# Gate stage of a hybrid decoder block: y transposed by DMA in 16-bit planes instead of by TensorE

## What is computed

```python
proj = hn @ w_in
q, k, v, z, xbc, dt_raw, gate_logits = jnp.split(proj, split_points, axis=-1)
...
y = ssd_chunked(...) + xs * d_skip
y = y * silu(z)                                  # (256 tokens, 4096)
yg = y.reshape(bsz, seq, 8, 512)                 # 8 groups
yg = yg * lax.rsqrt(jnp.mean(jnp.square(yg), axis=-1, keepdims=True) + EPS)
y = yg.reshape(...) * norm_w
y_ssm = y @ w_ssm_out                            # needs y transposed
gates = jax.nn.sigmoid(gate_logits)
h = h + (g_attn * y_attn + g_ssm * y_ssm) @ w_out
h = h + jnp.square(relu(rms_norm(h) @ w_up)) @ w_down
```

## Time and profile before

| what | us |
|---|---|
| median of 3 runs | 2055.06 (2054.35 to 2055.19) |
| profiled execution, its own time | 2054.75 |
| its span, first to last instruction | 2052.7 |
| TensorE busy | 2041.6 (99%) |
| VectorE, ScalarE, GpSimd busy | 1216.3, 1037.7, 189.4 |
| raw loads of w_in | 319 of 512 KB |

### The profile page before, as it was taken

How to read it: one execution, slowest core, us unless ns; L and a number is a source line. 1 busy time by engine, 2 the same in 40 slices (tenths; PEclk the granted TensorE clock), 3 DMA queues, 4 the chain that set the end, 5 groups by cost and what they waited for, 6 DMA issues and landing times.

```text
span 2052.7 us, 27154 instructions
## 1 busy us (share of the span) xinstructions
PE 2041.6 (99%) x9374; PEld 1694.7 (83%) x9374; DVE 1216.3 (59%) x1346; ACT 1037.7 (51%) x1238; POOL 189.4 (9%) x210
## 2 busy tenths in 40 slices
PE   9999999999999999999999999999999999999999
PEld 8888888888888888888888888888888888888887
DVE  5665566666666666666655555555545555554654
ACT  6454555555565454545554444455435534534542
POOL 2110010000012111111210000000000000000000
PEclk9999999999999999999999999999999999999999
DMA  7656555656665655666555556567667666666765
GB/s 241 186 164 183 166 167 171 178 176 179 178 201 177 194 194 184 196 198 190 174 183 185 193 187 225 194 185 223 203 193 211 213 193 202 204 210 194 201 218 163
DMA packets 231213, 394.08 MB, mean 192 GB/s; under 512 B 45776, under 2 KB 46736, under 8 KB 230880
## 3 DMA queue, kind: packets, MB, share of 16 engines
q1 hardware_dynamic: 229712, 389.54, 62.0%
q10 hardware_dynamic: 960, 2.75, 0.4%
q0 software_dynamic: 464, 0.77, 0.2%
HBM read 382.46 MB, written 2.16 MB: 187 GB/s over the span
## 4 chain that ended last, share of the span: by engine, by line
PE 97%; DVE 1%; ACT 1%; issue 0%; DMA 0%; DVEq 0%; ACTq 0%
PE ps L485 31%; PE ps L487 31%; PE ps L486 30%; PE ps L454 2%; PE ps L710 1%; ACT whi L849 0%; PE ps L562 0%; PE ps L539 0%; PE ps L699 0%; DVE f_st L1682 0%; DVE fT_lo L1690 0%; PE ps L720 0%; DVE cacc L1462 0%; ACT fT_hi L1236 0%; DVE wlo L1268 0%
## 5 line engine op out<-in xcount | busy, mean ns | idle before, releaser
L1268 DVE TENSOR_TENSOR wlo<-raw,whi 128x1024 fp32r<-128x1024 f32 x703 | 892.2, 1277 | 669.1 <-ACT whi L849 667.4
L849 ACT ACTIVATE whi<-raw 128x1024 fp32r<-128x1024 f32 x703 | 736.5, 1058 | 645.5 <-PE ps L487 628.6
L485 PE MATMUL ps<-whi,xT_hi 128*128 128x512 f32 x1276 | 509.5, 399 | 0.0
L487 PE MATMUL ps<-whi,xT_lo 128*128 128x512 f32 x1276 | 498.1, 390 | 0.0
L486 PE MATMUL ps<-wlo,xT_hi 128*128 128x512 f32 x1276 | 496.9, 389 | 0.0
L487 PEld LDWEIGHTS ps<-whi,xT_lo 128*128 128x128 f32 x1276 | 239.5, 188 | 51.3
L486 PEld LDWEIGHTS ps<-wlo,xT_hi 128*128 128x128 f32 x1276 | 240.0, 188 | 47.8 <-issue 1.0
L485 PEld LDWEIGHTS ps<-whi,xT_hi 128*128 128x128 f32 x1276 | 239.8, 188 | 47.8 <-issue 1.3
L485 PE MATMUL ps<-whi,fT_hi 128*128 128x512 f32 x512 | 199.6, 390 | 3.3 <-DVE fT_lo L1690 3.3
L485 PE MATMUL ps<-whi,hT_hi 128*128 128x512 f32 x512 | 199.3, 389 | 0.0
L487 PE MATMUL ps<-whi,fT_lo 128*128 128x512 f32 x512 | 199.2, 389 | 0.0
(11 more groups left out here) (254 smaller groups left out, 1856.7 us busy)
## 6 DMA issues: line engine op xcount, KB each, us to landing
raw<-in_w_in SPq DMA_DIRECT2D x319, 512.0 KB, 3.8
raw<-in_w_up SPq DMA_DIRECT2D x128, 512.0 KB, 4.1
raw<-in_w_down SPq DMA_DIRECT2D x128, 512.0 KB, 4.3
raw<-in_w_ssm_out SPq DMA_DIRECT2D x64, 512.0 KB, 4.2
raw<-in_w_attn_out SPq DMA_DIRECT2D x32, 512.0 KB, 4.3
raw<-in_w_out SPq DMA_DIRECT2D x32, 512.0 KB, 4.4
arow<-arows SPq DMA_DIRECT2D x16, 512.0 KB, 4.9
h<-in_x ACTq DMA_DIRECT2D x1, 2048.0 KB, 12.0
```

Source lines behind the costliest of these rows:

```text
L485: mm(dst, xh, whi[sl][:, kk, :], start=(s == 0 and kk == 0), stop=False)
L487: last = mm(dst, xl, whi[sl][:, kk, :], start=False, stop=(s == US - 1 and kk == UK - 1))
L849: A(whi[s % SLOTS][:, :, :], raw[s % SLOTS][:, :, :], ACT.Copy).then_inc(hi_ready, 1)
L1268: V.tensor_tensor(wlo[s % SLOTS][:, :, :], raw[s % SLOTS][:, :, :], fp(whi[s % SLOTS][:, :, :]), ALU.subtract).then_inc(lo_ready, 1)
```

## The change

The eight groups of y go the MLP's way. `y_halve(G)` on ScalarE copies the two 16-bit planes of xs[G] into `y_half`; `y_turn(G, a)` on SyncE transposes plane a into `y_tiles`; `y_join(G)` on VectorE puts the planes together into `yT`, from which `s_hi` and `s_lo` read, with the norm weights from `par`. There is one buffer of each, so `y_halve(G)` waits for both turns of group G - 1, a turn of G for the join of G - 1, and `y_join(G)` for the lo parts of G - 1.

Where they stand, with jb the gate block: ScalarE does s_hi(2jb - 1) and y_halve(2jb) in step 0, y_halve(2jb + 1) and s_hi(2jb) in step 4; VectorE s_lo(2jb - 1) in step 0, y_join(2jb) in step 3, s_lo(2jb) in step 5, y_join(2jb + 1) in step 7. SyncE issues the first turn of group 2jb behind the load of unit 7 of block jb, its second behind unit 0 of the next block, and both turns of group 2jb + 1 behind units 4 and 5 of that. TensorE's transposes and GpSimd's `y_copy` are gone. The gate blocks are written out instead of looped on ScalarE, VectorE and SyncE, and so is SyncE's first pair of SSM blocks.

```diff
@@ -142,3 +142,5 @@
         la = sb("la", "W", 1 * KB, [P, NTOK, SNH])
-        y_st = [sb(f"y_st{i}", "W", 4 * KB * i, [P, NTOK, GW]) for i in range(2)]
+        y_half = sb("y_half", "W", 0, [P, 2, NTOK, GW], u16)
+        y_tiles = sb("y_tiles", "W", 4 * KB, [P, 2, NTOK * 4, P], u16)
+        yT = sb("yT", "W", 8 * KB, [P, 4, T])
         blank = sb("blank", "W", 4 * KB, [P, P])
...
@@ -365,3 +367,21 @@
 
-            def load_block(b, w, row0, col0, turn=None):
+            def y_turn(G, a):
+                sp.wait_ge(y_halved, G + 1)
+                if G:
+                    sp.wait_ge(y_joined, G)
+                else:
+                    sp.wait_ge(ysq_done, 16)
+                sp.dma_start_transpose(y_tiles[:, a, :, :], y_half[:, a, :, :].rearrange("p t n -> p (t n)")) \
+                    .then_inc(y_turned, 16)
+
+            def gate_turns(jb, s):
+
+                if jb and s == 0:
+                    y_turn(2 * jb - 2, 1)
+                if jb and s in (4, 5):
+                    y_turn(2 * jb - 1, s - 4)
+                if jb < 4 and s == 7:
+                    y_turn(2 * jb, 0)
+
+            def load_block(b, w, row0, col0, gate=None, turn=None):
 
@@ -374,2 +394,4 @@
                         r_turn(turn, s - US + 2)
+                    if gate is not None:
+                        gate_turns(gate, s)
 
@@ -424,5 +446,7 @@
                 ssd_loads(j1)
-            with sp.Fori(0, 4) as j:
-                load_block(B_GATE + j, w_in, 0, GATE0 + D + j * COLS)
-            with sp.Fori(0, 4) as j:
+            for j in range(4):
+                load_block(B_GATE + j, w_in, 0, GATE0 + D + j * COLS, gate=j)
+            load_block(B_SSM, w_ssm_out, 0, 0, gate=4)
+            load_block(B_SSM + 1, w_ssm_out, D, 0)
+            with sp.Fori(1, 4) as j:
                 load_block(B_SSM + 2 * j, w_ssm_out, 0, j * COLS)
@@ -743,18 +767,5 @@
 
-            def y_transposes(G, i):
-                def f():
-                    pe.wait_ge(y_copied, G + 1)
-                    for c in range(4):
-                        for t in range(NTOK):
-                            o = (c % 2) * T + t * P
-                            last = transpose(ps[4 + 2 * i + c // 2][:, o:o + P], y_st[i][:, t, c * P:(c + 1) * P])
-                    last.then_inc(y_T, 1)
-                return f
-
             with pe.Fori(0, 2) as i:
                 for k in range(2):
-                    jb = 2 * i + k
-                    G = 2 * jb
-                    stream(B_GATE + jb, k, 18 + i, xT_hi, xT_lo,
-                           after={2: [y_transposes(G, 0)], 6: [y_transposes(G + 1, 1)]})
+                    stream(B_GATE + 2 * i + k, k, 18 + i, xT_hi, xT_lo)
 
@@ -1142,16 +1153,26 @@
 
-            def s_hi(G, i):
+            def y_halve(G):
+                def f():
+                    act.wait_ge(yfin, 2 * G + 2)
+                    if G:
+                        act.wait_ge(y_turned, 32 * G)
+                    else:
+                        act.wait_ge(y_mm, 16)
+                    A(y_half[:, :, :, :].rearrange("p a t n -> p a (t n)"),
+                      halves(xs[:, G, :, :].rearrange("p t n -> p (t n)")), ACT.Copy).then_inc(y_halved, 1)
+                return f
+
+            def s_hi(G):
                 def f():
-                    act.wait_ge(y_T, G + 1)
+                    act.wait_ge(y_joined, G + 1)
                     for c in range(4):
-                        A(sT_hi[:, bass.ds(4 * G + c, 1), :].rearrange("p a t -> p (a t)"),
-                          ps[4 + 2 * i + c // 2][:, (c % 2) * T:(c % 2 + 1) * T], ACT.Copy,
-                          scale=sw[i][:, c:c + 1]).then_inc(sT_hi_done, 1)
+                        kt = 4 * G + c
+                        A(sT_hi[:, kt, :], yT[:, c, :], ACT.Copy,
+                          scale=par[:, SSM_C + kt:SSM_C + kt + 1]).then_inc(sT_hi_done, 1)
                 return f
 
-            with act.Fori(0, 2) as i:
-                for k in range(2):
-                    jb = 2 * i + k
-                    steps(B_GATE + jb, {2: [s_hi(2 * jb, 0)], 6: [s_hi(2 * jb + 1, 1)],
-                                        7: [sgate_evac(B_GATE + jb, k, jb)]})
+            for jb in range(4):
+                steps(B_GATE + jb, {0: ([s_hi(2 * jb - 1)] if jb else []) + [y_halve(2 * jb)],
+                                    4: [y_halve(2 * jb + 1), s_hi(2 * jb)],
+                                    7: [sgate_evac(B_GATE + jb, jb % 2, jb)]})
 
@@ -1163,2 +1184,4 @@
                         act.wait_ge(m_step, 3 * j)
+                    else:
+                        act.wait_ge(y_turned, 32 * 8)
                     for t in range(NTOK):
@@ -1176,3 +1199,3 @@
 
-            steps(B_SSM, {7: [half_evac(0)]})
+            steps(B_SSM, {0: [s_hi(7)], 7: [half_evac(0)]})
             steps(B_SSM + 1)
@@ -1594,17 +1617,25 @@
 
-            def s_lo(G, i):
+            def y_join(G):
                 def f():
-                    for half in range(2):
-                        dve.wait_ge(sT_hi_done, 4 * G + 2 * half + 2)
-                        for cc in range(2):
-                            c = 2 * half + cc
-                            V.scalar_tensor_tensor(
-                                sT_lo[:, bass.ds(4 * G + c, 1), :].rearrange("p a t -> p (a t)"),
-                                ps[4 + 2 * i + half][:, cc * T:(cc + 1) * T], sw[i][:, c:c + 1],
-                                fp(sT_hi[:, bass.ds(4 * G + c, 1), :].rearrange("p a t -> p (a t)")),
-                                ALU.mult, ALU.subtract).then_inc(sT_lo_done, 1)
+                    dve.wait_ge(y_turned, 32 * G + 32)
+                    if G:
+                        dve.wait_ge(sT_lo_done, 4 * G)
+                    for a in range(2):
+                        i = V.tensor_copy(halves(yT[:, :, :].rearrange("p c t -> p (c t)"))[:, a, :],
+                                          y_tiles[:, a, :, :].rearrange("p (t c) l -> p c t l", t=NTOK))
+                    i.then_inc(y_joined, 1)
+                return f
+
+            def s_lo(G):
+                def f():
+                    for c in range(4):
+                        kt = 4 * G + c
+                        dve.wait_ge(sT_hi_done, kt + 1)
+                        V.scalar_tensor_tensor(sT_lo[:, kt, :], yT[:, c, :], par[:, SSM_C + kt:SSM_C + kt + 1],
+                                               fp(sT_hi[:, kt, :]), ALU.mult, ALU.subtract).then_inc(sT_lo_done, 1)
                 return f
 
-            with dve.Fori(0, 4) as jb:
-                steps(B_GATE + jb, {2: [s_lo(2 * jb, 0)], 6: [s_lo(2 * jb + 1, 1)]})
+            for jb in range(4):
+                steps(B_GATE + jb, {0: [s_lo(2 * jb - 1)] if jb else [], 3: [y_join(2 * jb)], 5: [s_lo(2 * jb)],
+                                    7: [y_join(2 * jb + 1)]})
 
@@ -1635,3 +1666,3 @@
 
-            steps(B_SSM)
+            steps(B_SSM, {0: [s_lo(7)]})
             steps(B_SSM + 1, {7: [merge_ssm(0)]})
@@ -1855,17 +1886,2 @@
 
-
-            def y_copy(Gn, i):
-                pool.wait_ge(yfin, 2 * Gn + 2)
-                G.tensor_copy(y_st[i][:, :, :], xs[:, bass.ds(Gn, 1), :, :].rearrange("p a t n -> p (a t) n"))
-                G.tensor_copy(sw[i][:, :], par[:, bass.ds(SSM_C + 4 * Gn, 4)]).then_inc(y_copied, 1)
-
-            pool.wait_ge(y_mm, 16)
-            pool.wait_ge(yz_done, 8)
-            y_copy(0, 0)
-            y_copy(1, 1)
-            with pool.Fori(1, 4) as j:
-                for i in range(2):
-                    pool.wait_ge(sT_lo_done, 8 * j - 4 + 4 * i)
-                    y_copy(2 * j + i, i)
-
```

More of the change, by code:

```diff
@@ L189, in build @@
         grs = small("grs", [P, 2])
-        sw = [small(f"sw{i}", [P, 4]) for i in range(2)]
         hss = small("hss", [P, NTOK, 4])
@@ L302, in build @@
         yfin = sem("yfin")
-        y_copied = sem("y_copied")
-        y_T = sem("y_T")
+        y_halved = sem("y_halved")
+        y_turned = sem("y_turned")
+        y_joined = sem("y_joined")
         sT_hi_done = sem("sT_hi_done")
```

## The result

The change took **2063.93 us** in the median of 6 runs (2061.73 to 2065.84), the kernel before beside it 2055.24 (6 runs, 2054.35 to 2056.58): a ratio of 1.004, 95% interval 1.003 to 1.0051. It is slower by 8.7 us, where 6.3 were forecast. The profiled execution took 2061.73, the fastest of the six. What follows splits up its 7.0 us over the profiled execution of before (7.3 by the spans); how far the median's remaining 2.2 us can be explained is said with the account of the prediction.

What follows compares the result with a forecast made beforehand. TensorE was taken to bound the kernel, 97% of a 2052.7 us span. From the profiled 2054.75 us, minus 7.2 for the transposes plus 13.9 of waits gave 2061.4 us, range 2051.5 to 2066.

Steps and rivals of the forecast that it cites:

- What is removed: TensorE in the gate stage loses 64 transposes, 7.23 us, all on the path.
- the ring: Gate-stage loop of waits over two groups through y_halve, turns, join and splits: 26.23 us against TensorE's 21.76 per block.
- The hi parts out of SBUF: On ScalarE, per group: four hi parts reading SBUF take 1.52 us, the middle of 1.45 and 1.60.
- The disputed term: On SyncE's queue: a second turn, issued 0.47 us behind a load, lands in 4.7 us.
- rival 1: A second turn lands like a lone one, 3.1 us; ring 23.0, waits 1.7, time 2049.2; chance 0.15.
- rival 2: A second turn lands at the median of all, 3.9 us; ring 24.6, waits 7.5, time 2055.0; chance 0.22.
- The waits: TensorE waits for wlo's split, gate blocks 1 to 3 and first SSM block: 2.35 + 8.9 + 2.6 = 13.9 us.
- 3: Rival: SyncE issues loads late; sign, ScalarE waits for raw; adds 6 us, time 2067.6; chance 0.06.

Runs made afterwards that it cites:

- experiment 3: The change without the sixteen turns: y_join reads y_half itself, so y is not transposed and the output differs; 2050.07 us, ratio 0.9977.
- experiment 2: The change with both turns of each group issued back to back, even group's behind unit 7's load, odd group's behind unit 4's; 2050.76 us, ratio 0.9979.
- experiment 1: The change with each second turn that followed a load issued just ahead of it, the load's lo_ready wait staying ahead of the turn; 2051.66 us, ratio 0.9985.
- The change's second profile: Profile from measuring the change again, unaltered; median of those runs 2064.77 us, ratio 1.0043 to the kernel before.
- experiment 4: The change with 64 transposes of the identity put back on TensorE into unused PSUM, results unused; 2062.08 us, ratio 1.0037.
- 5: The kernel of experiment 2 with TensorE's gate loop written out, same matmuls; 2050.28 us, ratio 0.9976.
- 7: The change with only the even groups' two turns issued together, behind unit 7's load; 2055.49 us, ratio 1.0002.
- 9: The kernel of experiment 2 with 36 instead of 4 warming matmuls at the start of TensorE's program; 2054.87 us, ratio 0.9997.
- 8: The change with only the odd groups' two turns issued together, behind unit 4's load; 2055.9 us, ratio 1.0005.

## Why the prediction was right, and where it was off

**What is removed, 7.23.** Right: experiment 3 has 87.0 us for the gate stage. The Trainium skill's 390 ns a transpose, given for bf16 (VectorE: DVE Perf Modes, The three transpose paths), would by estimate have made it 25; the measurement decides for 7.2. Its advice (Rules for kernel authors, on the same page) to stay on TensorE where PSUM will do holds for this change as it was made, for another reason than that figure: the ring, not the price of a transpose. With experiment 2, faster than before by 0.2%, it no longer holds here.

**The ring, 26.23 against 21.76.** Right, and 0.3 too long: 25.84 and 25.91 measured. By its parts: y_halve to the landing of the even second turn 9.36 (9.53 in the sum); from there to the join of the odd group 13.53 (13.77); to the next y_halve 3.02 (2.93). The hi parts out of SBUF took 1.60, the upper bound, not 1.52 (1028.31 to 1029.91). What made up for it: SyncE's load followed the start of VectorE's split by 1.25 and not 1.39, twice a ring, and the odd group's second turn reached the join 4.59 after its issue, not 4.75.

**The disputed term, 4.7.** Right: 4.5 to 4.7 against 3.1 of rival 1 and 3.9 of rival 2. The loads ahead of the turns do make them late. That experiment 1 then gives 12 us by moving only second turns over one load shows how much rests on it.

**The waits, 13.9.** Right in place and order, mis-sized by a little: 0.73 + 1.81 in the second block (2.35), 2.0 + 1.81 in the third (4.45), 2.0, 0.4 and a stretch at half the clock, 1.2, in the fourth (4.45), and 1.96 in the SSM stage (2.6). From start to start that is 11.9 us; 1.3 more are in small steps, for one since the matmul after a wait is followed after 0.31 and not 0.227. In all the two stages have 13.2 us over the pure stream, where 13.9 stood. The first matmul on sT_hi came at 1084.1, where 1084 stood. The first join came at 1000.61 and the second at 1014.10, where 999.99 and 1013.7 stood: the first two turns landed in 5.9 and 6.0, VectorE entered 0.6 sooner, and of the two errors 0.6 and 0.4 are left. Gate stage 3.7 for 4.1, SSM stage 2.2 for 2.6.

**What the sum lacked.** The MLP's 1.3 us, of which 0.9 are the gaps that the last section describes and 0.2 a longer first wait for fT_lo. The gate and SSM stages alone, 3.7 + 2.2, put the profiled execution at 2060.7, 0.7 under the forecast; the rest of the way to 2061.73 is the MLP. The median of the runs is 2.2 above the profiled one, which can't be split up as a whole. The change's second profile, 2065.29, shows what can differ: its 3.6 us more are a gate stage that begins 1.5 later, lasts 0.6 longer, and an MLP 1.5 longer. The 1.5 ahead of the gate stage are a stretch at half the clock near 620 us (the last section). The 0.6 are the ring: its first wait is 1.38 for 0.73, since the second turn of group 1 landed in 5.0 for 4.5. The MLP's are again gaps at the start of loop turns and longer first waits for fT_lo. I had named nothing that could change the MLP, since no line of it is changed; so the forecast's range holds the measured time because the ring was right, and 2.5 us between its 2061.4 and the median are terms that it did not have.

**Rivals.** 1 and 2 fall with the landings. 3 shows only as its first sign: ScalarE waited three times for a load, 4.2 in all, but only in the first SSM block, from 1097 us on, behind the last join and behind TensorE's last wait (1094.22); TensorE did not wait for it.

## What to carry to other kernels

A transpose taken off the busiest engine is worth its time only if what replaces it comes round in less than the step of the stream it feeds: draw the whole ring of waits, with the queue entries that stand between two of its transfers and what those wait for, and compare its length with that step. Transfers that one consumer needs together are best issued with nothing between them that waits. Here the place of one transfer in two, ahead of a 512 KB load instead of behind it, was worth 12 us (experiment 1); taking the load's wait for another engine from between them as well was worth 13 (experiment 2). The two are so close because either brings the ring nearly down to a block, and below that there is nothing left to gain. Where the ring is the longer one, the time of the engine freed is no gain, and most work put on it is free (5.6 of 7.2 us in experiment 4).

## What was not expected of the hardware

**TensorE's clock fell to half in the middle of the stream.** Windows of all engines, with the granted clock as the third column from the end:

```profile
1065.00:1069.00 4.00, 2.19 (x11) 1.51 (x10) 3.18 (x6) 1.78 (x5) 0.00 (x0) 1.00 0.42 136
1069.00:1073.00 4.00, 3.82 (x11) 2.50 (x9) 2.16 (x5) 4.00 (x4) 0.00 (x0) 0.59 0.76 186
1073.00:1076.00 3.00, 2.92 (x13) 2.43 (x14) 2.21 (x2) 1.52 (x2) 0.00 (x0) 0.98 0.63 171
```

and TensorE's timeline in the middle one:

```profile
1068.43 0.47 PE L509 MATMUL ps<-whi,xT_hi 128*128 128x512 f32 x1 [1.81 <-DVE wlo L1291]
...
1069.44 0.39 PE L510 MATMUL ps<-wlo,xT_hi 128*128 128x512 f32 x1
...
1071.76 0.63 PE L510 MATMUL ps<-wlo,xT_hi 128*128 128x512 f32 x1
1072.19 0.63 PE L511 MATMUL ps<-whi,xT_lo 128*128 128x512 f32 x1
1073.08 0.49 PE L509 MATMUL ps<-whi,xT_hi 128*128 128x512 f32 x1 [0.27 <-DVE wlo L1291]
```

After 1.81 us of waiting and 1.4 at full speed, matmuls come every 0.43 us instead of 0.227 until 1072.19, which is 1.2 GHz; by finer windows the granted clock is 0.50 from 1070.0 to 1073.0, 0.70 in the half microsecond before and 0.88 in the one after. It cost nothing here, since TensorE was ahead of the ring anyway: the next wait is 0.27, where the same one a block earlier was 1.65. The change's second profile has the same stretch at 1046.23, again behind one of these waits, with 0.29 at the next. The other waits of the same length have none.

It is not tied to the waits of this ring. The second profile has one more such stretch in the SSD stage, where the change touches nothing, behind a wait of 1.01 us and 16 small matmuls:

```profile
617.36 2.00 PE L734 MATMUL ps<-xf,M 128*128 128x64 f32 x16 [1.01 <-DVE M L1538]
...
620.09 0.63 PE L511 MATMUL ps<-whi,xT_lo 128*128 128x512 f32 x1
620.51 0.63 PE L509 MATMUL ps<-whi,xT_hi 128*128 128x512 f32 x1
```

There nothing hides it, and it costs 1.6 us. The profiles of before and of the first execution of the change have the same wait at that place and no such stretch. The profiles of before and of experiments 1 to 5 and 7 to 9 have none anywhere. The runs without a profile point the same way: of 62 runs of the kernel before that ran beside the experiments, the 52 with a mean granted clock of 1.000 took 2054.46 to 2055.90 us, the ten with 0.999 took 2056.21 to 2056.93. Of ten runs of the change, one has 1.000 and two 0.998; of the five of experiment 4, where TensorE waits 5.8 us and not 9.6, all have 1.000. So the waits may make such a stretch more frequent, and where it falls decides what it costs. What decides whether one comes stays open.

**TensorE loses time at the start of a turn of its loop in the MLP,** in part put down to "issue". From start to start the second and third turn begin late by 0.68 and 0.20 us in the change, 1.11 and 0.77 in its second profile, 0.50 and 0.68 in experiment 1, 0.77 and 0.25 in 2, 1.18 and 0.29 in 3, 0.48 and 0.60 in 7, 0.34 and 1.11 in 8; by nothing in before and in experiments 4, 5 and 9. It doesn't go with the turns of y or with waits for them: experiment 3 has none of these turns. The seven profiles that have it are all those in which TensorE's program ahead of this loop is only shorter by the transposes; in the four that don't, the transposes are there (before, 4), the gate loop is written out (5) or the start padded (9). That suggests the length of TensorE's program ahead of the loop. But the loss varies between two profiles of the same kernel, and the medians of experiments 2 and 5 differ by 0.5 only; what causes it is not shown.

**The first two turns of the stage took longest,** 5.9 and 6.0 us to land, where the later second ones took 4.5 to 4.7, the later first ones of even groups 3.0 (3.1 in the earlier trace rows) and those of odd groups 4.4 to 4.6.
